# Four slots of values moved between the first four query tiles and the fifth, with the memory tiles made behind the fourth head

## The reference, cut to what matters

```
h = rms_norm(x, a_norm);  q, k, v, qm, gate = split(h @ a_w_in)      # 768, 768, 768, 256, 1024 columns
q, k = partial_rope(rms_norm per head of 64)
kvm = rms_norm(mem, mem_norm) @ mem_w_kv;  km = rms_norm per head, vm # 256 memory tokens
o = softmax attention twice per head, p0 - lam * p1;  om = attention of qm over km, vm
x = x + (concat(o, om) * silu(gate)) @ a_w_out
```

## Time and profile before

| what | value |
|---|---|
| median of 3 runs | 2250.26 us (2249.25 to 2251.5) |
| the profiled execution | 2252.02 us, its span 2250.2 us |
| PE busy | 2175.5 us, 97% of the span |
| DVE, POOL, ACT busy | 1197.0, 1155.3, 935.5 us |

### The profile page before, as it was taken

One profiled execution on the slowest core, in us unless ns is written; L12 is line 12 of the kernel. 1 busy time (PEld: TensorE's weight loads), 2 busy tenths in 40 slices (PEclk: granted clock), 3 DMA queues, 4 the chain that ended last, 5 costly groups with the idle time before them and its releaser, 6 DMA issues.

```text
span 2250.2 us, 27312 instructions
## 1 busy us (share of the span) xinstructions
PE 2175.5 (97%) x9962; PEld 1686.0 (75%) x9962; DVE 1197.0 (53%) x1797; ACT 935.5 (42%) x1585; POOL 1155.3 (51%) x1360
## 2 busy tenths in 40 slices
PE   7999999999999999999999999799999999999998
PEld 5786588765776678888887888576688888877886
DVE  8968774568586340064167842673410432297642
ACT  4547633366454452232235522254432322237322
POOL 3563255631474235565565866172245654575852
PEclk9999999999999999999999999999999999999999
DMA  3232132311132123322332233131132333322321
GB/s 137 93 95 65 38 95 93 103 57 29 57 113 66 57 85 95 111 87 82 97 110 76 94 103 103 38 103 47 43 117 94 94 95 93 94 94 75 122 85 66
DMA packets 53126, 191.30 MB, mean 85 GB/s; under 512 B 6017, under 2 KB 6529, under 8 KB 52481
## 3 DMA queue, kind: packets, MB, share of 16 engines
q1 hardware_dynamic: 51696, 184.31, 26.1%
q10 hardware_dynamic: 1296, 5.24, 0.6%
HBM read 187.43 MB, written 2.10 MB: 84 GB/s over the span
## 4 chain that ended last, share of the span: by engine, by line
PE 80%; DVE 10%; ACT 4%; POOL 2%; DMA 2%; issue 2%; SPq 0%; DVEq 0%; ACTq 0%
PE proj L559 20%; PE proj L561 19%; PE proj L560 19%; PE score L555 5%; PE proj L555 4%; PE stat L555 3%; PE turned L555 2%; PE mix L555 2%; POOL lower L511 2%; DMA raw_ring<-stream 2%; PE ptp L787 1%; PE score L559 1%; PE score L561 1%; PE score L560 1%; DVE tmp L1716 1%
## 5 line engine op out<-in xcount | busy, mean ns | idle before, releaser
L511 POOL TENSOR_TENSOR lower<-raw_ring,upper 128x256 fp32r<-128x256 f32 x1340 | 1138.7, 883 | 1040.4 <-ACT upper L1202 1040.1
L559 PE MATMUL proj<-h,upper 128*128 128x512 f32 x1408 | 571.8, 406 | 7.8 <-DVE h L1721 3.1
L1202 ACT ACTIVATE upper<-raw_ring 128x1024 fp32r<-128x1024 f32 x335 | 350.6, 1057 | 545.9 <-PE proj L559 285.7
L561 PE MATMUL proj<-h,lower 128*128 128x512 f32 x1408 | 550.8, 391 | 0.0
L560 PE MATMUL proj<-h,upper 128*128 128x512 f32 x1408 | 549.9, 391 | 0.0
L559 PEld LDWEIGHTS proj<-h,upper 128*128 128x128 f32 x1408 | 265.5, 189 | 68.8 <-issue 9.3
L561 PEld LDWEIGHTS proj<-h,lower 128*128 128x128 f32 x1408 | 264.9, 188 | 56.7
L560 PEld LDWEIGHTS proj<-h,upper 128*128 128x128 f32 x1408 | 265.7, 189 | 52.6 <-issue 3.8
L559 PE MATMUL proj<-y,upper 128*128 128x512 f32 x586 | 233.1, 398 | 9.0 <-ACT qk L1306 5.7
L560 PE MATMUL proj<-y,upper 128*128 128x512 f32 x586 | 230.1, 393 | 0.0
L561 PE MATMUL proj<-y,lower 128*128 128x512 f32 x586 | 229.8, 392 | 0.0
(11 more groups left out here) (489 smaller groups left out, 3485.7 us busy)
## 6 DMA issues: line engine op xcount, KB each, us to landing
raw_ring<-stream SPq DMA_DIRECT2D x335, 512.0 KB, 3.5
landing<-stream SPq DMA_DIRECT2D x5, 512.0 KB, 9.8
x<-x_in SPq DMA_DIRECT2D x4, 512.0 KB, 6.8
rows<-rows_in ACTq DMA_DIRECT2D x2, 1024.0 KB, 5.3
out<-x SPq DMA_DIRECT2D x8, 256.0 KB, 2.0
memraw<-mem_in SPq DMA_DIRECT2D x1, 1024.0 KB, 13.1
memraw<-mem_in ACTq DMA_DIRECT2D x1, 1024.0 KB, 4.9
rot<-tables_in ACTq DMA_DIRECT2D x2, 512.0 KB, 3.6
```

The costliest lines, as they stand in the source:

```text
L511: ins = nc.gpsimd.tensor_tensor(lower[:, p % RING, a:b], slot_source(p)[:, a:b], upper[:, p % RING, a:b].bitcast(FP32), ALU.subtract)
L559: first_ = nc.tensor.matmul(o, lhsT[0], rhs[0], start=start, stop=False)
L561: return first_, nc.tensor.matmul(o, lhsT[1], rhs[0], start=False, stop=stop)
L1202: nc.scalar.activation(upper[:, p % RING, :], slot_source(p), ACT.Copy).then_inc(split_upper, 1)
```

## The change

The four 512-column value slots come ahead of tile 4. The sums of tiles 1, 2 and 3 stand behind the first, second and third of them, and from tile 5 on the sums run one tile behind the products. The last sum stands behind the first 256-column slot. ACT roots the memory's mean and takes the four values between root(2) and tile 4, DVE makes the memory tiles between normalise(2) and rotate(4). Values use ptp, turned, proj0 and proj1; the narrow ones use score0, score1, ptp and turned.

```diff
+EARLY_BANKS = (4, 6, 0, 1)
@@ first_stream
-    out = names("a.q", MT) + names("a.k", MT) + names("a.qm", 2) + names("a.v", 6) + mem(0)
+    out = names("a.q", 4) + names("a.v", 4) + names("a.q", MT)[4:] + names("a.k", MT) + names("a.qm", 2) + ["a.v4", "a.v5"] + mem(0)
@@ PE, tokens
-                    o = (token_bank(j0 + b, b) if not places else lru_bank(0, places[b]))[:, 0:width]
+                    o = (token_bank(j0 + b, b) if not places else lru_bank(places[b], places[b]))[:, 0:width]
@@ PE, heads
                 memory_squares(0, KT)
-                summed()
-                jobs[4]()
-                summed()
-                i0 = 5
+                middle(summed)
+                i0 = 4
...
-                if i and (i < len(jobs) or last):
+                if i > i0 and (i < len(jobs) or last):
                     summed()
@@ PE, layer a
-                                  together=lambda: group(S, C, W, names("a.q", 4), h, hkey, (0, 0, 0, 1)), last=False)
-                tokens(S, C, W, names("a.v", 4), h, hkey, 512, TB, places=FREE_BANKS,
-                       behind=([(0, 3), (1, 2)], last_sums))
-                tokens(S, C, W, ["a.v4", "a.v5"], h, hkey, 256, TB)
+                                  together=lambda: group(S, C, W, names("a.q", 4), h, hkey, (0, 0, 0, 1)), last=False,
+                                  middle=lambda summed: tokens(S, C, W, names("a.v", 4), h, hkey, 512, TB, places=EARLY_BANKS,
+                                                               behind=([(0, 3), (1, 3), (2, 3)], summed)))
+                tokens(S, C, W, ["a.v4", "a.v5"], h, hkey, 256, TB, places=FREE_BANKS, behind=([(0, 3)], last_sums))
@@ ACT, heads (ahead of next_job of tile i)
+                if together and i == 4:
+                    middle()
@@ ACT, middle
+        def memory_root_and_values():
+            act.wait_ge(*S.after("mem_sums"))
...
+                .then_inc(*S.mark("rooted", ("mem_root",)))
+            for b in range(TB):
+                take(S, C, v1[:, b, 0:512], bank_=lru_bank(EARLY_BANKS[b], EARLY_BANKS[b]))
+            feed(wanted[0])
@@ DVE, rotated_heads
                 if i > 1:
                     normalise(i - 1)
+                if i == 3:
+                    middle()
@@ DVE, middle (the same instructions as stood behind lam_rows)
+        def memory_tiles():
...
+            for k in range(KT):
+                mem_tile(0, k)
```

More of the change, by code:

```diff
@@ L716, in added_squares, with heads @@
                     .then_inc(*S.mark("summed", ("sq_used", i), *([("sums", m)] if i == t else [])))
-        def heads(S, C, W, jobs, cols=SEQ, together=None, between=None, last=True):
+        def heads(S, C, W, jobs, cols=SEQ, together=None, between=None, last=True, middle=None):
             def summed():
@@ L1273, in root_ended, with heads @@
                 nc.scalar.activation(square, std[:, m % 2, 0:cols], ACT.Square, scale=scale).then_inc(*S.mark("rooted", ("std_sq", m)))
-        def heads(S, C, n, cols=SEQ, together=False, between=None, gains=()):
+        def heads(S, C, n, cols=SEQ, together=False, between=None, gains=(), middle=None):
             for i in range(n + 1):
@@ L1413, in act_program @@
         tables()
+        def memory_root_and_values():
+            act.wait_ge(*S.after("mem_sums"))
+            nc.scalar.activation(mem_inv[:, :], mix[:, 0:MEM], ACT.Ln, bias=small[:, 0:1], scale=1.0 / DM)\
+                .then_inc(*S.mark("rooted", ("mem_ln",)))
+            act.wait_ge(*S.after("mem_ln"))
+            nc.scalar.activation(mem_inv[:, :], mem_inv[:, :], ACT.Exp, scale=-0.5)\
+                .then_inc(*S.mark("rooted", ("mem_root",)))
+            for b in range(TB):
+                take(S, C, v1[:, b, 0:512], bank_=lru_bank(EARLY_BANKS[b], EARLY_BANKS[b]))
+            feed(wanted[0])
         for l, s in enumerate("ab"):
@@ L1416, in act_program @@
                 act.wait_ge(*S.after("key_gains"))
[L1417 to L1423, removed]
+                heads(S, C, 2 * MT + 2, together=True, gains=[fc("a_q")] * MT + [fc("a_k")] * MT, middle=memory_root_and_values)
             else:
@@ L1436, in act_program @@
                         root(S, C, 1.0 / HD, MEM, half=1)
-            for a, z in ((0, 512), (512, 768)) if s == "a" else ((512, 768), (0, 512)):
+            for a, z in ((512, 768),) if s == "a" else ((512, 768), (0, 512)):
                 for b in range(TB):
                     take(S, C, v1[:, b, a:z], cols=z - a, keys_=[("values_ready", s)], block=b, later=s == "b" and z - a == 256,
-                         bank_=lru_bank(0, FREE_BANKS[b]) if s == "a" and a == 0 else None)
+                         bank_=lru_bank(0, FREE_BANKS[b]) if s == "a" else None)
                 feed(wanted[0])
@@ L1778, in add_square, with rotated_heads @@
                  ("sq_used", t), *([("sq_used", t - 1)] if i == 1 else []), *([("added", tag)] if i == KT - 3 else []))
-        def rotated_heads(S, C, dsts, ready, plain, gains, plain_ready):
+        def rotated_heads(S, C, dsts, ready, plain, gains, plain_ready, middle):
             n0, turned_ = C.n["head"], len(dsts)
@@ L1977, in mem_tile @@
             norm_tile(S, mh[:, k, :, :], memraw[:, k, :], fc("mem_norm", 8 * l + k), mem_inv[:, :], MEM, ("h", f"mem{l}", k))
+        def memory_tiles():
+            dve.wait_ge(mem_loaded, 16)
+            dve.wait_ge(*S.after("mem_root"))
+            w = tmp[:, 0:MEM]
+            link(S, nc.vector.tensor_scalar(w, mix[:, 0:MEM], -0.5 / DM, -0.5 * EPS, ALU.mult, ALU.add))
+            link(S, nc.vector.tensor_tensor(w, w, mem_inv[:, :], ALU.mult))
+            link(S, nc.vector.tensor_tensor(w, w, mem_inv[:, :], ALU.mult))
+            link(S, nc.vector.scalar_tensor_tensor(out=mem_inv[:, :], in0=w, scalar=1.5, in1=mem_inv[:, :], op0=ALU.add,
+                                                   op1=ALU.mult))
+            for k in range(KT):
+                mem_tile(0, k)
         for l, s in enumerate("ab"):
@@ L1982, in dve_program @@
                               [("qk_ready", s)] * (2 * MT), [qm[:, t, :] for t in range(2)], [fc("mem_q", l)] * 2,
-                              [("heads_ready", s)] * 2)
+                              [("heads_ready", s)] * 2, memory_tiles)
                 C.n["job"] += 2 * TB
@@ L1989, in dve_program @@
                 link(S, nc.vector.tensor_scalar(small[:, 13:14], fc("subln"), 1.0 - LAMBDA_INIT, None, ALU.mult))
[L1990 to L1999, removed]
                 dve.wait_ge(*S.after("lam_exps"))
```

## The result

The changed kernel has a median of 2253.89 us in 20 runs, the kernel before 2250.84 in 20 runs beside it. The ratio is 1.0014, with a 95% interval of 1.0008 to 1.0020: +3.1 us (1.8 to 4.5), where +0.5 was forecast. One run of each kernel lay far out (3414.47 us before, 8131.7 after) and is left out of the ratio. The median lies in the range, and within the 0.2% called no change. But the interval lies wholly above 1: the prediction held that less than 0.2% can't be told from no change, and 20 runs of each do tell it, as a small loss. The first profiled span is 2251.4 us. The first sum of squares does not start at the same time in every execution (46.75 us in the kernel before, 46.03 after, 45.89 to 48.60 over all profiles), so in what follows I subtract that start where two kernels are compared.

What follows compares the result with a forecast made beforehand. PE, busy 97% of the span, was taken as the bound. Removing 6.4 us and adding 6.9 us (5.0 us wait, 1.86 us slow clock) gave +0.5 us on 2250.26, so 2250.8 us; range 2246.5 to 2255.0 us.

Steps and rivals of the forecast that it cites:

- the 0.2% called no change: Whole kernel: a change of less than 0.2%, 4.5 us, can't be told from none.
- What is removed: PE's stretch 47 to 176 us: waits of 0.75, 3.05 and 0.78 us and 1.86 us slow clock go, 6.4 us.
- ACT in its feed: Ahead of tile 4: PE waits 5.0 us for proj0 while ACT feeds four slots before copying the values.
- DVE's memory tiles: Between normalise(2) and rotate(4): tiles take 19.5 us, done at 89.0; half_var(3) at 92.7, hidden by 0.8 us.
- from both sides then sum(4) begins at about 93: At sum(4): without PE's wait for ACT, PE would ask at 86.6 and get half_var(3) at 92.7.
- The slow clock: Half clock behind PE's wait: 1.86 us removed behind the old 3.05 us wait, 1.86 us added behind the new one.
- Lambda's rows: At lambda's matmul, about 157.7 us: moving the last sum and lam_rows costs 0 to +0.5 us, taken as 0.
- Attention's start: Early memory tiles and earlier memory-key slots may shorten attention's start by tenths; taken as 0, other end -0.5 us.
- a sign of being wrong: No wait at 75.6, a second at sum(4) above 1 us, or attention starting more than 3 us from its place.

Runs made afterwards that it cites:

- fix_waits: takes_tiles_lag, but ACT's feed catches up one slot at tile 12 and ACT copies the narrow values ahead of its feed; ratio to before 1.0010.
- takes_first: The changed kernel, but ACT feeds slots 8 and 9, takes the four values, then feeds slots 10 and 11; ratio to before 1.0015.
- keys_first: The changed kernel, but ACT copies and squares each memory key ahead of its feed; ratio to before 1.0012.
- lam_early: The changed kernel, but DVE makes lambda's rows ahead of the early memory tiles; run once, 2253.97 us.
- takes_tiles_lag: takes_tiles, but ACT's feed ahead of a tile stops one slot earlier from tile 4 on; ratio to before 1.0013.
- takes_tiles: takes_first, but only four memory tiles behind normalise(2), two behind normalise(11) and two behind normalise(12); ratio to before 1.0002.
- tiles_late: The changed kernel with the memory tiles back behind all heads; ratio to before 1.0062 in two runs.

## Why the prediction was right, and where it was off

- **What is removed.** Shown by the profile: the waits of 0.7, 3.1 and 0.6 us and the slow clock behind the second are gone, and none comes at sums 1 to 3. fix_waits, which has no new wait up to lambda's matmul, is there 6.9 us sooner than the kernel before; 6.4 was the forecast for what is removed.
- **ACT in its feed.** Right in place, releaser and size: 5.18 us against 5.0. takes_first shows that the feed causes it, since the wait at tile 4 goes when the copies stand ahead of the feed.
- **DVE's memory tiles.** Right in length: 19.3 us against 19.5. That half_var(3) came 0.8 us ahead of PE, as forecast, is luck: the forecast had it wait for the memory tiles, but in the run DVE was idle for 1.89 us behind them, since PE at half clock ended tile 4 late and ACT copied it late; and PE's sum(4) was late by the same clock. The path that was forecast is the one of takes_first: half_var(3) lets PE go 94.60 - 48.60 = 46.0 us after the first sum, against 92.7 - 46.75 = 45.95. So the claim that "from both sides then sum(4) begins at about 93" holds: without ACT's hold the time stays.
- **The slow clock, mis-sized.** The term of the sum was 1.86 us. 48 matmuls at 0.227 us are 10.9 us, tile 4 and 5 took 13.86, so it was 3.0, 1.1 us more. And the 1.86 itself was read across two views: 61.60 is a start of PE's timeline, 69.81 one of the chain of waits, and the timeline has that sum at 69.65 (the row below). It took 69.65 - 61.60 = 8.05 us, so the old slow clock cost 1.7 us. The term stands on both sides of the sum, so this did not move the forecast; it makes what was removed 0.16 us smaller.

```profile
69.65 1.02 PE L555 MATMUL stat<-sq,const 128*128 128x512 f32 x2
```

- **Lambda's rows, mis-sized.** I took 0 of "0 to +0.5"; the matmul waited 0.34 us. At it, measured from the first sum, the kernel is 112.51 - 110.62 = 1.9 us behind the one before.
- **Attention's start, mis-sized.** I took 0, with a gain at the other end. It lost 1.2 us: 3.88 us of ACT's hold for slot 24 stand ahead of the copy of the first memory key, and PE waits 1.16 us for the second key's square. keys_first shows that this hold is not all: without it 0.3 us come back, and PE waits at the next sum instead. At a score of attention (178.85 after, 176.50 before) the kernel is 132.82 - 129.75 = 3.1 us behind, at the edge of what the prediction named as a sign of being wrong (attention more than 3 us from its place; without the first sum subtracted it is 2.35).

The forecast of 0.5 with 0.2 for the wait, 1.1, 0.16, 0.3 and 1.2 makes 3.5, against 3.1 at the score in the profiles and 3.1 (1.8 to 4.5) in the runs; the other 0.4 is not accounted for. All these misses point the same way, and the wide range took them in. That profile and runs agree to a tenth is chance, too. Behind the score the distance of the two profiles stays for long: at one matmul (413.99 after, 411.45 before) it is 3.3 us. Just behind it the kernel before runs for some us at half clock and the changed one doesn't (windows below, the kernel before first), and by the end the spans differ by (2251.4 - 46.03) - (2250.2 - 46.75) = 1.9 us only.

```profile
421.00:425.00 4.00, 4.00 (x12) 3.12 (x11) 0.00 (x0) 1.92 (x3) 2.00 (x3) 0.57 0.28 111
```

```profile
421.00:425.00 4.00, 3.20 (x14) 2.67 (x15) 0.75 (x1) 2.03 (x3) 1.42 (x3) 1.00 0.34 109
```

keys_first and lam_early did not show the two small terms in the time, and in their profiles most of what one frees is taken by the next wait; so the two terms say where the changed kernel loses time, not what their removal would win. That the gain of 6.4 us is used up by the hold and its slow clock is shown by takes_tiles_lag, which takes both away and wins 8.3 us up to that point.

Why these 8.3 us could not be kept I had not seen at all. Slots pass the DMA, ACT and POOL in turn through two raw buffers, and the stretch up to attention has slots that PE uses up faster (the narrow values and the memory keys, 5.8 and 2.9 us each, against 6.35 for a head). PE sooner there means slots wanted sooner, and a hold of ACT's feed turns up ahead of whichever copy stands next: narrow values, keys, exponentials. The runs show the hold at five places in turn: ahead of the value copies, of tile 4's copy, of the narrow values, of the memory keys and of the exponentials. That more raw buffers would end it is only argued; it was not tried. Nor was another order of the banks: tile 4 goes to proj0, which ACT empties third of the four. Taken first, proj0 would come free some 0.95 us sooner (an estimate from the copies at 78.60 and 79.55), and DVE's hold stands close behind.

## What to carry to other kernels

When a blocking feed stands in an engine's own order, look at every copy that the change puts behind it, and price it by the same sequence elsewhere in the trace. Walk the path of each engine to the next common point: two holds that end there together mean that the removal of one shows nothing. A gain inside a stretch counts only when the supply behind the stretch can follow; nearly every removal here moved the wait on to the next copy, root or tile. Take both ends of a difference from one view: a chain of waits and a timeline give different starts for the same instruction.

## What was not expected of the hardware

The stretch at half clock behind a pause of PE is not of one size, and does not follow the length of the pause. By how much later than at full clock the next sum came (PE's timeline; 6.35 us from sum to sum, 10.9 us from tile 4 to sum(4)), in one execution each:

| kernel | pause, us | slow clock cost, us |
|---|---|---|
| before | 3.05 | 1.7 |
| takes_tiles | 4.08 | 1.5 |
| tiles_late | 4.29 | 1.6 |
| lam_early | 5.15 | 1.7 |
| changed, two profiles | 5.18, 5.19 | 3.0, 2.9 |
| keys_first | 5.29 | 1.5 |
| takes_first | 6.16 | 2.3 |

The rows show part of the difference. In the kernel before the clock was 1.00 throughout the pause, and matmuls became slow only at 63.02, 1.4 us after PE had gone on. In the changed kernel it was 0.92 over the pause, so it had fallen before PE went on, and stayed low until about 86.3.

The spread of 1.5 to 3.0 us may be why the changed kernel's times scatter more (2250.15 to 2256.36, apart from one outlier) than those of the kernel before (2249.13 to 2252.16, likewise). The clock has a part in the scatter: the nine runs of the changed kernel with a mean granted clock of 0.989 over the span took 2255.0 us on average, the nine with 0.990 took 2253.3, the one with 0.991 took 2250.15. Whether the stretch behind this wait makes the difference is not shown.
